# A three-layer transformer block on one core: the feed-forwards' first products computed by features, with the weights held stationary and 256 tokens moving

## The chip, the core and the metric

The kernel runs on one core of a Trainium2 chip. Five engines run side by side: PE (TensorE, matrix products into PSUM), DVE (VectorE) and ACT (ScalarE) for elementwise work, POOL (GpSimd) and SP (SyncE, which issues most DMAs here). They meet by semaphores alone. The metric is the time of one launch on the device, in microseconds (us). Several launches are timed and their median is given; one more launch was profiled.

## The reference

The input is 256 tokens of width 1024. Two layers of feed-forward, mixer (latent attention in one, forgetting attention in the other), feed-forward and gated embedding are followed by a block of dilated attention and pooling. The change touches the four feed-forwards alone:

```python
def rms_norm(x, g):
    y = x * lax.rsqrt(jnp.mean(x * x, axis=-1, keepdims=True) + EPS)
    return y * g

def swiglu(x, w_in, w_out):
    gate, up = jnp.split(x @ w_in, 2, axis=-1)
    return (jax.nn.silu(gate) * up) @ w_out

h = h + FFN_HALF * swiglu(rms_norm(h, g_ffn), w_in, w_out)   # w_in 1024 x 5632, w_out 2816 x 1024
```

Everything is in single precision. The kernel gets it from the fast format fp32r: each operand is split into a rounded part (hi) and the remainder (lo), and a product is the sum of hi·hi, hi·lo and lo·hi, three matmuls into one accumulator.

## The kernel before, in words

The program is written out by hand, engine by engine, with a table (`PLAN`) that numbers every weight group and every fill of an accumulator. Weights come in groups of 1 MB: SP fetches group g into `raw[:, g % 4]`, ACT rounds it into `wh` (L1328), DVE subtracts to get `wl` (L1809), and PE reads both. These two passes over each group run through the whole kernel in a ring of four slots.

A feed-forward (`ffn` on each engine) has 11 chunks of 256 gate and 256 up features, two groups each. The normalized input stands transposed in `xh` and `xl`: eight blocks of 128 features by 256 tokens. The row scale of the norm, `rstd`, one number per token, isn't in it; it is applied to the products.

For each chunk PE takes the tokens as the stationary operand (`tall_group`, L593 to L595):

```python
mm = products(acc(q, t)[:, 0:n], ah_[:, k0 + k, t * P:(t + 1) * P],
              al_[:, k0 + k, t * P:(t + 1) * P],
              wh[:, s, k * n:(k + 1) * n], wl[:, s, k * n:(k + 1) * n],
```

So 8 blocks x 2 token halves x 3 products = 48 matmuls stream 512 weight columns each, and `acc(q, t)` holds 128 tokens by 256 gate and 256 up values. ACT makes `sg` = silu(gate · rstd) per half (L1411), DVE makes `a_n` = up · rstd · sg (L1960). The second product needs `a_n` with features on the partitions, so in the middle of the next chunk PE turns it by four 128x128 transposes into `misc` (`turn_products`, L668); ACT rounds the result into `ah` (L1417) and DVE subtracts for `al` (L1967). After the last chunk the wide stage multiplies `ah` and `al` by `w_out` (L593 to L595 in its first chunk, then L626, L627, L630).

Accumulators alternate: chunk c+2 fills the banks of chunk c, after `acc_read` tells that DVE has read them. On DVE and ACT the order in a chunk is written out: split of a group, remainder (or rounding) of the chunk before, split of the next group, then the activation work, which waits for PE's end of the chunk. The first chunks are written out (3 in the first feed-forward, 1 in the others) and the rest run in a hardware loop of two chunks.

Elsewhere in the kernel there are fp32r matmuls with other numbers of moving columns: 288 and 384 in the latent attention, and 256 with a stationary operand of 16 columns for the forget gates (L1068, L1071, L1072).

Of the kernel before, what the change touches and what calls it, by code (L numbers as in the profile page):

```python
# [76 lines left out]
def plan():  # L77
# [1 line left out]

    sizes = {  # L80
        "norm": (0, 0, (1, 1, 1, 1), (4, 4, 4, 4)),
        "ffn": (33, 13, (6, 5, 0, 0), (6, 5, 0, 0)),
        "ffn_t": (33, 13, (6, 5, 0, G3), (6, 5, 0, G3)),
        "ffn_p": (33, 13, (6, 5, 1, 0), (6, 5, 1, 0)),
        "mla": (14, 12 + H, (H // 2 + 2, H // 2 + 2, H + 2, H + 1), (H + 2, H + 2, H + 2, H + 1)),
        "fox": (17, 9, (H, H, H, H + 3), (H, H, H, H + 3)),
        "ple": (5, 4, (0, 0, 0, 0), (0, 0, 0, 0)),
# [72 lines left out]
def build(nc, I, out):  # L160
    with ExitStack() as ctx:
# [182 lines left out]
        rstd_done = sem("rstd_done")  # L344
        xh_done = sem("xh_done")
        silu_done = sem("silu_done")
        ah_done = sem("ah_done")
        gate_done = sem("gate_done")
        lat_sq = sem("lat_sq")
# [40 lines left out]
        def acc_reads(q):  # L390

            return 2 * (q // 2) + 2
# [168 lines left out]

        TURN_AT = {"n1": 4}
        FIRST_SILU = {"f0": 0, "f1": 1, "f2": 2, "f3": 3}
        OH = {"mla": 0, "fox": 4, "b2": 4 + PAIRS}


        @block.tensor
        def _(pe):
# [146 lines left out]
            def ffn(name, nname, r, after, r_after, with_p=None):  # L715
# [13 lines left out]
                def turn_products(c, i=0):  # L729

                    b, q = c % 2, q0 + c
                    pe.wait_ge(acc_read[q % 2], acc_reads(q) + 2 * i)
                    if r0[b] + c // 2 > 0:
                        pe.wait_ge(m_read[b], r0[b] + c // 2 + i)
                    for t in range(NT):
                        for k in range(2):
                            mm = turn(b, slice(k * S + t * P, k * S + (t + 1) * P),
                                      a_n[:, b, t, k * P:(k + 1) * P])
                    mm.then_inc(m_ready[b], 1)

                peel = 3 if g0 == 0 else 1
                first_fill(nname, r, g0, q0)
                for c in range(1, peel):
                    chunk(c)
                with pe.Fori(0, (FCH - peel) // 2) as i:
                    for c in range(2):
                        chunk(peel + c, i)
                q, g = q0 + FCH, g0 + 2 * FCH
                for c in range(FCH):
                    wait_group(g + c)  # L750
                    pe.wait_ge(m_read[c % 2], r0[c % 2] + c // 2 + 1)
                    if c == 0:
                        wide_first(g, q, ah, al)
                    else:
                        for t in range(NT):
# [550 lines left out]
        def _(act):  # L1306
# [95 lines left out]
            def ffn(name, r):  # L1402
                g0, q0, f0, _ = PLAN[name]

                def silus(c, i=0):
                    q, g = q0 + c, g0 + 2 * c + 1
                    for t in range(NT):
                        tile_ready(act, q, t, g, i, 2)
                        if c == 0:
                            scaled(r, t)  # L1410
                        act.activation(sg[:, c % 2, t, :], acc(q, t)[:, 0:256], ACT.Silu,  # L1411
                                       scale=rstd[:, t:t + 1]).then_inc(silu_done, 1)

                def round_a(c, i=0):
                    b = c % 2
                    act.wait_ge(m_ready[b], f0[b] + c // 2 + 1 + i)
                    act.activation(ah[:, bass.ds(i * 4 + 2 * c, 2), :],  # L1417
                                   M[:, b, :].rearrange("p (k n) -> p k n", k=2), ACT.Copy).then_inc(ah_done, 1)

                peel = 3 if g0 == 0 else 1  # L1420
                for c in range(peel):
                    split_to(g0 + 2 * c + 3)
                    if c:
                        round_a(c - 1)
# [6 lines left out]
                with act.Fori(0, (FCH - peel) // 2) as i:  # L1431
                    for c in range(peel, peel + 2):
# [355 lines left out]
        def _(dve):  # L1788
# [161 lines left out]

            def ffn(name, r, after):

                g0, q0, f0, _ = PLAN[name]
                base = FIRST_SILU[name] * FCH

                def gated(c, i=0):
                    q = q0 + c
                    for t in range(NT):
                        dve.wait_ge(silu_done, NT * (base + c) + t + 1 + 4 * i)
                        dve.scalar_tensor_tensor(a_n[:, c % 2, t, :], acc(q, t)[:, 256:512], rstd[:, t:t + 1],  # L1960
                                                 sg[:, c % 2, t, :], ALU.mult, ALU.mult)\
                           .then_inc(acc_read[q % 2], 1)

                def rest_a(c, i=0):
                    b = c % 2
                    dve.wait_ge(ah_done, base + c + 1 + 2 * i)
                    dve.tensor_tensor(al[:, bass.ds(i * 4 + 2 * c, 2), :], pair(M[:, b, :]),  # L1967
                                      ah[:, bass.ds(i * 4 + 2 * c, 2), :].bitcast(F32), ALU.subtract)\
                       .then_inc(m_read[b], 1)

                peel = 3 if g0 == 0 else 1
                for c in range(peel):
                    split_to(g0 + 2 * c + 3)
                    if c:
                        rest_a(c - 1)
# [4 lines left out]
                with dve.Fori(0, (FCH - peel) // 2) as i:  # L1980
                    for c in range(peel, peel + 2):
# [775 lines left out]
```

## Time and profile before

| what | value |
|---|---|
| median of 3 launches | 1351.64 us (1349.71 to 1352.4) |
| the profiled launch's own time | 1351.75 us |
| its span in the trace | 1349.9 us |
| PE busy | 1325.5 us, 98% of the span, 6514 matmuls |
| weight loads of PE (PEld) | 1092.0 us, 6514 |
| DVE busy | 789.1 us, 58% |
| ACT busy | 672.6 us, 50% |
| DMA | 236.46 MB, 175 GB/s on average |
| granted TensorE clock, mean | 0.997 |

The durations of matmuls are modelled and overlap each other, so PE's speed is read from the distance between the starts of neighbours, not from "busy" or from the mean length of one. PEld is the loading of the stationary operand, which runs beside the matmul before it. A line of the code is that of the helper in which the instruction is made: L593 to L595 are every "three products" of the kernel, L668 is every transpose, and the names tell them apart.

### The profile page before, as it was taken

The numbers are of one execution on the slowest core, as the hardware profiler recorded it, in microseconds if no ns is written. First come the engines' busy times: TensorE is split into PE (matmuls) and PEld (weight loads), VectorE is DVE, ScalarE is ACT, GpSimd is POOL, SyncE is SP. The second block draws the span as 40 slices with busy tenths as digits, with TensorE's granted clock in tenths as the row PEclk, the third lists the DMA queues.
The fourth block names the chain that finished last, engine by engine and source line by source line (L and its number), as shares of the span: only waits on it lengthen the run. The fifth ranks groups of instructions, "written<-read, shape, count | busy, mean of one in ns | idle before, by whom it ended". The sixth has DMA issues, their size and how long they took to land.

```text
span 1349.9 us, 17526 instructions
## 1 busy us (share of the span) xinstructions
PE 1325.5 (98%) x6514; PEld 1092.0 (81%) x6514; DVE 789.1 (58%) x1013; ACT 672.6 (50%) x945; POOL 148.2 (11%) x207
## 2 busy tenths in 40 slices
PE   9999999899999999999999999999999999999996
PEld 6888788788888887888888788888888788888875
DVE  6655548875555546655545566655554645655663
ACT  7444427756444436544434555544443735457441
POOL 2000003811000000000001230000000132110500
PEclk9999999999999999999999999999999999999999
DMA  9655545235655654555554643465564495545531
GB/s 301 211 186 186 187 153 181 79 128 179 190 184 186 220 176 156 185 183 187 184 197 156 219 156 123 135 187 186 186 218 157 156 303 176 160 133 172 186 126 32
DMA packets 148782, 236.46 MB, mean 175 GB/s; under 512 B 10087, under 2 KB 103447, under 8 KB 148208
## 3 DMA queue, kind: packets, MB, share of 16 engines
q1 hardware_dynamic: 143680, 222.52, 50.6%
q0 software_dynamic: 4736, 12.96, 3.2%
q8 instruction: 40, 0.66, 0.2%
q10 hardware_dynamic: 304, 0.14, 0.1%
q14 instruction: 22, 0.18, 0.0%
HBM read 233.43 MB, written 4.51 MB: 176 GB/s over the span
## 4 chain that ended last, share of the span: by engine, by line
PE 85%; DVE 7%; ACT 3%; issue 2%; DMA 1%; POOL 1%; SPq 0%; POOLq 0%; DVEq 0%; ACTq 0%
PE acc L593 19%; PE acc L595 18%; PE acc L594 18%; PE acc L626 7%; PE acc L627 7%; PE acc L630 7%; PE misc L668 5%; DVE wl L1809 2%; ACT wh L1328 1%; ACT xh L1372 1%; PE misc L1018 1%; DMA decay<-decay_rows 1%; PE misc L1186 1%; DVE xl L1853 1%; PE misc L1205 1%
## 5 line engine op out<-in xcount | busy, mean ns | idle before, releaser
L1809 DVE TENSOR_TENSOR wl<-raw,wh 128x2048 fp32r<-128x2048 f32 (+2 forms) x203 | 458.7, 2267 | 265.6 <-ACT wh L1328 265.5
L1328 ACT ACTIVATE wh<-raw 128x2048 fp32r<-128x2048 f32 (+2 forms) x207 | 388.9, 1890 | 138.7 <-PE acc L630 130.3
L593 PE MATMUL acc<-wh,xh 128*128 128x512 f32 (+1 forms) x832 | 328.9, 395 | 2.7 <-DVE xl L1853 1.4
L595 PE MATMUL acc<-wh,xl 128*128 128x512 f32 (+1 forms) x832 | 323.2, 388 | 0.0
L594 PE MATMUL acc<-wl,xh 128*128 128x512 f32 (+1 forms) x832 | 322.6, 388 | 0.0
L593 PEld LDWEIGHTS acc<-wh,xh 128*128 128x128 f32 x832 | 156.3, 188 | 36.6 <-DVE wl L1802 4.2
L595 PEld LDWEIGHTS acc<-wh,xl 128*128 128x128 f32 x832 | 156.2, 188 | 32.7
L594 PEld LDWEIGHTS acc<-wl,xh 128*128 128x128 f32 x832 | 156.5, 188 | 30.0
L626 PE MATMUL acc<-wh,ah 128*128 128x512 f32 x320 | 125.7, 393 | 0.0
L627 PE MATMUL acc<-wl,ah 128*128 128x512 f32 x320 | 124.6, 389 | 0.0
L2541 POOL TENSOR_SCALAR rstd<-ssq 128x1 f32<-128x1 f32 x20 | 9.5, 476 | 905.2 <-ACT hn L1360 905.1
L1417 ACT ACTIVATE ah<-misc 128x512 f32 (+1 forms) x44 | 26.3, 598 | 156.0 <-PE misc L668 156.0
L593 PE MATMUL acc<-wh,zh 128*128 128x512 f32 x256 | 102.8, 401 | 0.8 <-DVE zl L1853 0.8
L595 PE MATMUL acc<-wh,zl 128*128 128x512 f32 x256 | 100.4, 392 | 0.0
L594 PE MATMUL acc<-wl,zh 128*128 128x512 f32 x256 | 100.2, 392 | 0.0
L630 PE MATMUL acc<-wh,al 128*128 128x512 f32 x320 | 98.6, 389 | 0.0
L1411 ACT ACTIVATE sg<-acc,rstd 128x256 f32<-128x256 f32 x88 | 41.4, 475 | 100.6 <-PE acc L595 100.6
L1967 DVE TENSOR_TENSOR al<-misc,ah 128x512 f32 (+1 forms) x44 | 30.4, 692 | 84.0 <-ACT ah L1417 84.0
L1372 ACT ACTIVATE xh<-misc,gains 128x128 fp32r<-128x128 f32 x128 | 40.3, 364 | 69.2 <-PE misc L668 60.1
L626 PEld LDWEIGHTS acc<-wh,ah 128*128 128x128 f32 x320 | 60.1, 188 | 13.8 <-issue 1.7
L630 PEld LDWEIGHTS acc<-wh,al 128*128 128x128 f32 x320 | 60.1, 188 | 12.7
L627 PEld LDWEIGHTS acc<-wl,ah 128*128 128x128 f32 x320 | 60.1, 188 | 12.2
(346 smaller groups left out, 1688.3 us busy)
## 6 DMA issues: line engine op xcount, KB each, us to landing
raw<-in_ffn_w_in_dram SPq DMA_DIRECT2D x172, 512.0 KB, 4.7
raw<-in_ffn_w_out_dram SPq DMA_DIRECT2D x88, 512.0 KB, 4.4
raw<-in_w_in_dram SPq DMA_DIRECT2D x64, 512.0 KB, 4.8
raw<-in_fox_w_in_dram SPq DMA_DIRECT2D x24, 512.0 KB, 4.5
raw<-in_ple_w_gate_dram SPq DMA_DIRECT2D x16, 512.0 KB, 4.1
raw<-in_mla_w_o_dram SPq DMA_DIRECT2D x8, 512.0 KB, 4.4
raw<-in_fox_w_o_dram SPq DMA_DIRECT2D x8, 512.0 KB, 4.4
raw<-in_w_out_dram SPq DMA_DIRECT2D x8, 512.0 KB, 4.5
```

What stands on the lines that cost most here:

```text
L593: pe.matmul(dst, hi, rhs_h, start=first, stop=False)
L594: pe.matmul(dst, hi, rhs_l, start=False, stop=False)
L595: return pe.matmul(dst, lo, rhs_h, start=False, stop=last)
L626: pe.matmul(acc(q + n, t), xa, wh[:, s, r], start=st, stop=False)
L627: pe.matmul(acc(q + n, t), xa, wl[:, s, r], start=False, stop=False)
L630: mm = pe.matmul(acc(q + n, t), xb, wh[:, s, r], start=False, stop=en)
L668: return pe.transpose(M[0:rows, b, cols], src, m[:, :])
L1328: act.activation(wh[:, s, 0:n], raw[:, s, 0:n], ACT.Copy).then_inc(hi_done, 1)
L1372: act.activation(x_cols(xh, r, k, t), turned(r, k, t), ACT.Copy, scale=gains[:, c:c + 1]).then_inc(xh_done, 1)
L1411: act.activation(sg[:, c % 2, t, :], acc(q, t)[:, 0:256], ACT.Silu, scale=rstd[:, t:t + 1]).then_inc(silu_done, 1)
L1809: dve.tensor_tensor(wl[:, s, 0:n], raw[:, s, 0:n], wh[:, s, 0:n].bitcast(F32), ALU.subtract)\
L1967: dve.tensor_tensor(al[:, bass.ds(i * 4 + 2 * c, 2), :], pair(M[:, b, :]), ah[:, bass.ds(i * 4 + 2 * c, 2), :].bitcast(F32), ALU.subtract)\
```

## The change

In each feed-forward, chunk 0 stays as it was. Chunks 1 to 10 swap the operands: a 128x128 block of `wh` or `wl` is stationary and `xh` or `xl` streams its 256 tokens. `acc(q, 0)` then holds 256 gate features (two blocks of 128) by 256 tokens and `acc(q, 1)` the up features, so the products already stand as the second product needs them. The row scale lies along the moving direction now. PE makes a row of it once per feed-forward, as two matmuls of `rstd`, broadcast to 128 columns, with the identity; DVE copies that to `rrow`. DVE scales the gate into `sg`, ACT takes the silu of `sg` in place, DVE scales the up part into `a_n` and multiplies the two; `ah` and `al` come from `a_n` directly. All four feed-forwards write out three chunks ahead of the loop on PE, ACT and DVE.

```diff
-        "ffn": (33, 13, (6, 5, 0, 0), (6, 5, 0, 0)),
+        "ffn": (33, 13, (1, 1, 0, 0), (1, 1, 0, 0)),
...
+        PEEL = 3
+        rrow = hn[:, 0, 0:S]
...
                 def chunk(c, i=0):
                     q, g = q0 + c, g0 + 2 * c
                     open_acc(q, i)
-                    for k in range(2):
-                        wait_group(g + k, i)
-                        tall_group(g + k, q, xh, xl, 4 * k, 4, 512, k == 0, k == 1)
-                        if k == 0:
-                            turn_products(c - 1, i)
+                    for n in range(2):
+                        wait_group(g + n, i)
+                        s = (g + n) % RING
+                        for k in range(4):
+                            x = 4 * n + k
+                            for b in range(4):
+                                dst = acc(q, b // 2)[:, (b % 2) * S:(b % 2 + 1) * S]
+                                w = slice(512 * k + P * b, 512 * k + P * (b + 1))
+                                pe.matmul(dst, wh[:, s, w], xh[:, x, :], start=x == 0 and b % 2 == 0, stop=False)
+                                pe.matmul(dst, wh[:, s, w], xl[:, x, :], start=False, stop=False)
+                                mm = pe.matmul(dst, wl[:, s, w], xh[:, x, :], start=False,
+                                               stop=x == DK - 1 and b % 2 == 1)
+                                if x == DK - 1 and b == 1:
+                                    mm.then_inc(acc_ready, 1)
+                        mm.then_inc(w_used, 1)
+                        if c == 1 and n == 0:
+                            turn_products()
+                            scales_by_token()
...
+                def scales_by_token():
+                    pe.wait_ge(rstd_done, NT * r + NT)
+                    open_m(1, r0[1])
+                    for t in range(NT):
+                        mm = pe.matmul(M[:, 1, t * P:(t + 1) * P], rstd[:, t:t + 1].to_broadcast([P, P]), ident[:, :],
+                                       start=True, stop=True)
+                    mm.then_inc(m_ready[1], 1)
...
-                    if c == 0:
-                        turn_products(FCH - 1)
...
 # ACT
+                    if c:
+                        act.wait_ge(gate_scaled, at + c + 2 * i)
+                        act.activation(sg[:, c % 2, :, :], sg[:, c % 2, :, :], ACT.Silu).then_inc(silu_by_feature, 1)
+                        return
...
+                    if c:
+                        act.wait_ge(a_done, at + c + 2 * i)
+                        act.activation(ah[:, bass.ds(i * 4 + 2 * c, 2), :], a_n[:, c % 2, :, :], ACT.Copy)\
+                           .then_inc(ah_done, 1)
+                        return
...
 # DVE
+                    if c == 1:
+                        dve.wait_ge(m_ready[1], f0[1] + 1)
+                        dve.tensor_copy(rrow, M[:, 1, 0:S]).then_inc(m_read[1], 1)
+                        dve.wait_ge(m_read[1], r0[1] + 1)
+                    tile_ready(dve, q, 0, g0 + 2 * c + 1, i, 2)
+                    dve.tensor_tensor(sg[:, c % 2, :, :], pair(acc(q, 0)), by_block, ALU.mult).then_inc(gate_scaled, 1)
+                    tile_ready(dve, q, 1, g0 + 2 * c + 1, i, 2)
+                    dve.tensor_tensor(a_n[:, c % 2, :, :], pair(acc(q, 1)), by_block, ALU.mult)\
+                       .then_inc(acc_read[q % 2], 2)
+                    dve.wait_ge(acc_read[q % 2], acc_reads(q) + 2 * i)
+                    dve.wait_ge(silu_by_feature, at + c + 2 * i)
+                    dve.tensor_tensor(a_n[:, c % 2, :, :], a_n[:, c % 2, :, :], sg[:, c % 2, :, :], ALU.mult)\
+                       .then_inc(a_done, 1)
...
+                    if c:
+                        dve.tensor_tensor(lo, a_n[:, c % 2, :, :], hi, ALU.subtract).then_inc(al_done, 1)
```

How it stands on PE in the middle of chunk 1 of a feed-forward, before (L668 turns the products of chunk 0):

```order
L595 MATMUL acc<-wh,xl 128x512
L668 MATMUL misc<-ident,a_n 128x128 x4
L593 MATMUL acc<-wh,xh 128x512
L594 MATMUL acc<-wl,xh 128x512
L595 MATMUL acc<-wh,xl 128x512
```

and of the change, at the same place (names are stationary last: `acc<-xh,wh` has `wh` stationary):

```order
L748 MATMUL acc<-xh,wl 128x256
L682 MATMUL misc<-ident,a_n 128x128 x4
L772 MATMUL misc<-ident,rstd 128x128 x2
L746 MATMUL acc<-xh,wh 128x256
L747 MATMUL acc<-xl,wh 128x256
L748 MATMUL acc<-xh,wl 128x256
```

The four transposes stand in every chunk from 1 on before, and once more in the wide stage; of the change they stand here alone, with two matmuls for the scale row behind them, and a chunk holds 96 matmuls of 256 columns in place of 48 of 512.

How it stands on DVE in one chunk of the loop, before:

```order
L1809 TENSOR_TENSOR wl<-raw,wh 128x2048 [waits hi_done]
L1966 REGISTER_ALU
L1967 ISA [waits ah_done]
L1967 TENSOR_TENSOR al<-misc,ah 128x512
L1808 REGISTER_ALU
L1809 TENSOR_TENSOR wl<-raw,wh 128x2048 [waits hi_done]
L1960 SCALAR_TENSOR_TENSOR a_n<-acc,rstd,sg 128x256 [waits silu_done] x2
```

and of the change:

```order
L1849 TENSOR_TENSOR wl<-raw,wh 128x2048 [waits hi_done]
L2025 ISA [waits ah_done]
L2025 TENSOR_TENSOR al<-a_n,ah 128x512
L1848 REGISTER_ALU
L1849 TENSOR_TENSOR wl<-raw,wh 128x2048 [waits hi_done]
L403 REGISTER_ALU
L2011 TENSOR_TENSOR sg<-acc,hn 128x512 [waits acc_ready]
L2013 TENSOR_TENSOR a_n<-acc,hn 128x512 [waits w_used]
L2015 REGISTER_ALU
L2017 TENSOR_TENSOR a_n<-a_n,sg 128x512 [waits silu_by_feature,acc_read0]
```

The two gated products of 256 elements have become three operations of 512, and the last of them waits for ACT, which itself waits for the first; the splits stand where they stood.

## Rows read from the trace of the kernel before

**Rows 1.** The page: busy time by engine, and the chain that ended last, by engine.

```profile
PE 1325.5 (98%) x6514; PEld 1092.0 (81%) x6514; DVE 789.1 (58%) x1013; ACT 672.6 (50%) x945; POOL 148.2 (11%) x207
...
PE acc L593 19%; PE acc L595 18%; PE acc L594 18%; PE acc L626 7%; PE acc L627 7%; PE acc L630 7%; PE misc L668 5%; DVE wl L1809 2%; ACT wh L1328 1%; ACT xh L1372 1%; PE misc L1018 1%; DMA decay<-decay_rows 1%; PE misc L1186 1%; DVE xl L1853 1%; PE misc L1205 1%
```

**Rows 2.** Timeline of PE, loop of feed-forward 0: start us, length us, line, op, names, count.

```profile
60.85 0.39 PE L595 MATMUL acc<-wh,xl 128*128 128x512 f32 x1
61.08 0.60 PE L668 MATMUL misc<-ident,a_n 128*128 128x128 f32 x4
...
61.75 0.39 PE L594 MATMUL acc<-wl,xh 128*128 128x512 f32 x1
...
83.81 0.60 PE L668 MATMUL misc<-ident,a_n 128*128 128x128 f32 x4
```

**Rows 3.** Timeline of PE, 512 moving columns: first and last of 29 in a row.

```profile
99.73 0.39 PE L593 MATMUL acc<-wh,xh 128*128 128x512 f32 x1
...
106.08 0.39 PE L594 MATMUL acc<-wl,xh 128*128 128x512 f32 x1
```

**Rows 4.** Timeline of PE, 384 columns (39 in a row) in latent attention.

```profile
227.03 0.33 PE L593 MATMUL acc<-wh,lh 128*128 128x384 f32 x1
...
233.62 0.33 PE L595 MATMUL acc<-wh,ll 128*128 128x384 f32 x1
```

**Rows 5.** Timeline of PE, 288 columns: second and last of 36 in a row.

```profile
202.16 0.29 PE L594 MATMUL acc<-wl,xh 128*128 128x288 f32 x1
...
206.69 0.29 PE L595 MATMUL acc<-wh,xl 128*128 128x288 f32 x1
```

**Rows 6.** Timeline of PE, forget gates: 256 columns, 16 stationary, first and last of 24.

```profile
733.62 0.28 PE L1068 MATMUL acc<-xh,wh 128*16 128x256 f32 x1
...
736.31 0.28 PE L1072 MATMUL acc<-xh,wl 128*16 128x256 f32 x1
```

**Rows 7.** Timeline of weight loads (PEld) in the last block's attention.

```profile
1225.74 1.86 PEld L1209 LDWEIGHTS misc<-qkv,pT 128*128 128x128 f32 x16
```

**Rows 8.** Groups by form: count | busy us, mean ns of one | idle before.

```profile
L1809 DVE TENSOR_TENSOR wl<-raw,wh 128x2048 fp32r<-128x2048 f32 x196 | 448.7, 2297 | 259.2 <-ACT wh L1328 259.1
...
L594 PEld LDWEIGHTS acc<-wl,xh 128*128 128x128 f32 x832 | 156.5, 188 | 30.0
...
L1960 DVE SCALAR_TENSOR_TENSOR a_n<-acc,rstd,sg 128x256 f32<-128x256 f32 x88 | 42.1, 483 | 26.8 <-ACT sg L1411 26.8
...
L1967 DVE TENSOR_TENSOR al<-misc,ah 128x512 f32 x38 | 26.3, 692 | 75.8 <-ACT ah L1417 75.8
...
L1417 ACT ACTIVATE ah<-misc 128x512 f32 x38 | 22.7, 598 | 137.4 <-PE misc L668 137.4
...
L1817 DVE TENSOR_TENSOR wl<-raw,wh 128x512 fp32r<-128x512 f32 x12 | 8.1, 678 | 0.0
```

**Rows 9.** Busy time by engine in one chunk: us, PE, PEld, DVE, ACT, POOL (counts), clock, DMA.

```profile
55.70:67.00 11.30, 11.30 (x54) 9.35 (x53) 6.21 (x5) 5.16 (x5) 0.00 (x0) 1.00 0.62 192
```

**Rows 10.** Timeline of DVE over a chunk of the loop; idle before in brackets.

```profile
79.07 0.48 DVE L1960 SCALAR_TENSOR_TENSOR a_n<-acc,rstd,sg 128x256 f32<-128x256 f32 x1 [0.20 <-ACT sg L1411]
80.87 2.29 DVE L1809 TENSOR_TENSOR wl<-raw,wh 128x2048 fp32r<-128x2048 f32 x1 [1.32 <-ACT wh L1328]
...
89.74 0.48 DVE L1960 SCALAR_TENSOR_TENSOR a_n<-acc,rstd,sg 128x256 f32<-128x256 f32 x1 [0.48 <-ACT sg L1411]
```

**Rows 11.** Timeline of DVE behind chunk 1 of feed-forward 0.

```profile
34.04 0.87 DVE L1960 SCALAR_TENSOR_TENSOR a_n<-acc,rstd,sg 128x256 f32<-128x256 f32 x2
...
36.73 2.29 DVE L1809 TENSOR_TENSOR wl<-raw,wh 128x2048 fp32r<-128x2048 f32 x1
```

**Rows 12.** Timeline of PE in the middle of chunk 2 of feed-forward 0.

```profile
38.70 0.48 PE L593 MATMUL acc<-wh,xh 128*128 128x512 f32 x1
```

**Rows 13.** The page: the queue that fetches PE's instructions.

```profile
q8 instruction: 40, 0.66, 0.2%
```

**Rows 14.** Chain of waits, in order of time: start us, us, what.

```profile
528.80 1.58 issue
```

More of the change, by code:

```diff
@@ L346, in build @@
         silu_done = sem("silu_done")
+        gate_scaled = sem("gate_scaled")
+        silu_by_feature = sem("silu_by_feature")
+        a_done = sem("a_done")
+        al_done = sem("al_done")
         ah_done = sem("ah_done")
@@ L735, in turn_products @@
+                def turn_products():
+                    pe.wait_ge(acc_read[q0 % 2], acc_reads(q0))
+                    open_m(0, r0[0])
                     for t in range(NT):
                         for k in range(2):
[L737 to L741, printed above, removed]
+                            mm = turn(0, slice(k * S + t * P, k * S + (t + 1) * P), a_n[:, 0, t, k * P:(k + 1) * P])
+                    mm.then_inc(m_ready[0], 1)
@@ L742, in ffn @@
+                def scales_by_token():
[5 more added lines that the diff above has]
+                    mm.then_inc(m_ready[1], 1)
                 first_fill(nname, r, g0, q0)
-                for c in range(1, peel):
+                for c in range(1, PEEL):
@@ L744, in ffn @@
                     chunk(c)
-                with pe.Fori(0, (FCH - peel) // 2) as i:
+                with pe.Fori(0, (FCH - PEEL) // 2) as i:
                     for c in range(2):
-                        chunk(peel + c, i)
+                        chunk(PEEL + c, i)
                 q, g = q0 + FCH, g0 + 2 * FCH
@@ L1430, in ffn @@
                         act.activation(cs[:, :, :, :], rc[:, :, :, :], ACT.Sin).then_inc(sines, 1)
-                with act.Fori(0, (FCH - peel) // 2) as i:
-                    for c in range(peel, peel + 2):
+                with act.Fori(0, (FCH - PEEL) // 2) as i:
+                    for c in range(PEEL, PEEL + 2):
                         split(g0 + 2 * c + 2, i)
@@ L1951, in ffn @@
             def ffn(name, r, after):
-                g0, q0, f0, _ = PLAN[name]
-                base = FIRST_SILU[name] * FCH
+                g0, q0, f0, r0 = PLAN[name]
+                base, at = FIRST_SILU[name] * FCH, by_feature(name)
+                by_block = rrow.unsqueeze(1).to_broadcast([P, 2, S])
                 def gated(c, i=0):
                     q = q0 + c
[L1958 to L1962, printed above, removed]
+                    if c == 0:
+                        for t in range(NT):
+                            dve.wait_ge(silu_done, NT * FIRST_SILU[name] + t + 1)
+                            dve.scalar_tensor_tensor(a_n[:, 0, t, :], acc(q, t)[:, 256:512], rstd[:, t:t + 1],
+                                                     sg[:, 0, t, :], ALU.mult, ALU.mult)\
+                               .then_inc(acc_read[q % 2], 1)
+                        return
+                    if c == 1:
[11 more added lines that the diff above has]
+                       .then_inc(a_done, 1)
@@ L1964, in rest_a @@
                 def rest_a(c, i=0):
-                    b = c % 2
                     dve.wait_ge(ah_done, base + c + 1 + 2 * i)
[L1967 to L1972, printed above, removed]
+                    hi = ah[:, bass.ds(i * 4 + 2 * c, 2), :].bitcast(F32)
@@ L1973, in ffn @@
+                    lo = al[:, bass.ds(i * 4 + 2 * c, 2), :]
+                    if c:
+                        dve.tensor_tensor(lo, a_n[:, c % 2, :, :], hi, ALU.subtract).then_inc(al_done, 1)
+                    else:
+                        dve.tensor_tensor(lo, pair(M[:, 0, :]), hi, ALU.subtract).then_inc(m_read[0], 1)
+                for c in range(PEEL):
                     split_to(g0 + 2 * c + 3)
@@ L1979, in ffn @@
                         (angles_reduced, head_constants, rope_tables)[c]()
-                with dve.Fori(0, (FCH - peel) // 2) as i:
-                    for c in range(peel, peel + 2):
+                with dve.Fori(0, (FCH - PEEL) // 2) as i:
+                    for c in range(PEEL, PEEL + 2):
                         split(g0 + 2 * c + 2, i)
```

33 lines of the change are left out of this document (14 added, 19 removed).

## The prediction

> **What bounds the kernel now.** I read the page first: PE is busy for 98% of the span and DVE for 58%, and the chain that ended last is almost only PE's lines, products first and transposes (L668) with 5% [rows 1]. So an edit in the feed-forwards counts by what it does to PE's time there, as long as DVE and ACT stay hidden. Second, the timeline of PE in a loop: turns of products follow each other two chunks apart at 61.08 and 83.81 us, which makes 11.365 us a chunk [rows 2], and no idle time stands beside them. Third, the cadence of matmuls, start to start. 28 steps of 512 columns take 6.35 us, 226.8 ns each [rows 3]. Fourth, the same for narrower ones, since the change issues 256. Last, DVE and ACT in one chunk: 6.21 and 5.16 us of work in 11.3 us [rows 9].
>
> **Part 1: transposes removed.** From the last matmul before a turn (60.85) to the second behind it (61.75) are 0.90 us [rows 2]; two steps of 0.227 would be 0.454, so four transposes cost PE 0.446 us, all of it on the path. Each feed-forward has 11 such turns and keeps one. 40 x 0.446 = 17.8 us go.
>
> **Part 2: the products.** Chunks 1 to 10 of four feed-forwards have 40 x 48 = 1920 matmuls of 512 columns and get 40 x 96 = 3840 of 256. The streamed columns are the same. What isn't the same is the piece of a step that doesn't scale with columns. Three forms with a full 128-column stationary operand show it:
> - 512 columns: 226.8 ns [rows 3]
> - 384 columns: 6.59 us over 38 steps, 173.4 ns [rows 4]
> - 288 columns: 4.53 us over 34 steps, 133.2 ns [rows 5]
>
> From 512 down to 384 the slope is 0.417 ns a column, on to 288 0.419; 32 columns less give 133.2 - 13.4 = 119.8 ns at 256. No column is saved, and some 13 ns of fixed cost are paid twice as often. No row has 256 fp32r columns on 128 stationary ones, so I bound it. From below: the forget gates stream 256 columns of the same `xh` and `xl` over only 16 stationary columns, 23 steps in 2.69 us, 117.0 ns [rows 6]; a full weight load can't be cheaper. From above: 16 weight loads of 128 columns stand in 1.86 us where the matmuls between are short; less the last one's 0.19, 15 steps of 111.5 ns are what a stream of loads takes by itself [rows 7]. That is under 119.8, so loads alone don't bind. If the 13.1 ns that 119.8 stands over its columns (256 at 0.417, 106.7) came on top of the load instead of the columns, it would be 111.5 + 13.1 = 124.6. The length of a load record, 188 ns [rows 8], is no bound: the same loads already follow each other every 133.2 ns [rows 5]. I take 119.8, since it is the same kind of instruction and the extrapolation is over 32 columns.
>
> A chunk is then 96 x 0.1198 = 11.50 us against 11.365 with its transposes: +0.136 us, over 40 chunks +5.4 us.
>
> The Trainium skill has a rule here, "TensorE: Matmul & The Clock Gate", section "Back-to-back issue gap": an isolated step takes N/2.4 + 2.5 ns. By it a 256-column step would be 109.2 ns. The trace disagrees already at 512 columns (215.8 by the rule, 226.8 measured) and at 256 with a small load (109.2 against 117.0), so the measured cadence decides; it is among the rivals below for what it would do.
>
> **Part 3: the scale row.** Two matmuls per feed-forward in the code, in plain fp32. Such a matmul runs as two: L1209 makes 8 calls at a time, and rows 7 show 16 loads. At the 0.112 us of rows 7 each, that is 4 x 4 x 0.112 = 1.8 us on PE. The copy to `rrow` is DVE's.
>
> **Part 4: DVE and ACT.** DVE's chunk before is 2 x 2.297 + 2 x 0.483 + 0.692 = 6.25 us [rows 8], 6.21 by the window [rows 9]. Now two scalings out of PSUM (0.692 each, like L1967), a product and a remainder from SBUF (0.678, like L1817): 4.59 + 1.38 + 1.36 = 7.3 us of 11.5. ACT trades two silus and a rounding for one of each over 512, about 0.6 each: no more than its 5.16. Both are costed at nothing; their cover is PE's 11.5 us, and without it the extra 1.1 us of DVE would be 44 us over 40 chunks.
>
> The new handoff is DVE, ACT, DVE at a chunk's end. Before, the last gated product ends about 1.2 us behind PE (a second half at 79.07 + 0.48 where the chunk ends near 78.35), and the next split starts at 80.87 only because ACT's does [rows 10]. Now: gate scaled while PE finishes the up part, silu 0.6, up scaled 0.69, product 0.68: done some 1.9 us behind PE, and the split behind it is again held by ACT's. The split that PE needs at the next chunk but one start is over 6 us early, so nothing reaches PE. The banks are free about 1 us after the chunk; they are wanted a whole chunk later, in the wide stage after its first 12 matmuls, 2.7 us.
>
> The tightest place is feed-forward 0, where DVE also makes constants. Behind chunk 1 its gated work is 0.87 us at 34.04 and the next split starts at 36.73 [rows 11]. The row copy (up to 0.5), two scalings, the wait for the silu and the product make it about 3.2, so that split ends near 41.3 in place of 39.02. Chunk 3 needs it at 38.70 + 24 x 0.227 + 0.09 = 44.2 [rows 12]. Hidden by 3 us. SP's fetches follow the splits; the group of 1 MB that they bring is wanted no faster than before.
>
> **Sum.** 5.4 + 1.8 = +7.2 us on the profiled launch's 1351.75: 1359.0. The median of the launches is 0.1 lower, so 1358.9 us. As a formula, with s the 256-column step in ns: 3.84 s - 452.8 us. It is zero at 117.9 ns; one nanosecond is 3.84 us. A measurement of this kernel can tell about 0.2%, 2.7 us, so steps of 117.2 to 118.6 ns give no difference.
>
> **Rivals.**
> - *A, the step is cheaper (117.0 to 117.2 ns), faster.* The place is PE's step in chunks 1 to 10; the fixed cost would shrink as the streaming part does. For it: the 117.0 of rows 6, and that 14 ns over the columns at 512 (226.8 - 213.3) are 13.4 at 384 and 13.2 at 288, so it falls a little. Against: rows 6 has a load of 16 columns. At 117.0: -3.5 us, 1348.1. It decides from 117.9 down. Chance 0.12, with whatever else the removed transposes set free. With a step of 109.2, the figure of the Trainium skill's TensorE page cited above, the time would be 33 us less, 1318; the two measured steps leave that 1 in 100 of these 12.
> - *B, between,* 117.2 to 118.6: 1349 to 1354.3. Chance 0.13.
> - *C, the weight load or its issue becomes the bound,* 124.6 ns: +25.7 us, 1377.3. For it: loads and streams are now both near 107 to 112 ns, so neither hides much of the other, and no row has more than 24 such steps in a row. Against: rows 7 hold 111.5 with full loads. Chance 0.05.
> - *D, the loop's branch costs.* The loop body on PE is 384 loads and matmuls in place of 208. For: a longer way back. Against: 0.66 MB of instructions were fetched in 40 packets [rows 13] while 13028 loads and matmuls ran, so loops weren't fetched again. The Trainium skill, "Runtime: NRT & Kernel Launch", section "Instruction fetch mechanics", says that a taken branch to a page no longer held stalls, but that PE holds 2048 instructions; no run here shows the size. At a stall like the longest "issue" piece of the chain between two DVE steps, 1.58 us [rows 14], 16 iterations give +25 more: 1384. Chance 0.03.
> - *E, the handoff reaches PE,* in feed-forward 0 or where a bank opens: it decides once DVE is over 3 us later than worked out; 1 us in each feed-forward gives 1363, 1 us in each chunk 1399. Chance 0.02.
>
> **How the numbers follow.** The forecast, a step of 118.6 to 121.5, has 0.65 and its own range of 1354.3 to 1365.4. Slower by over 0.2%: 0.65 + 0.05 + 0.03 + 0.02 = 0.75. Within 0.2%: B, 0.13. Faster: A, 0.12. The range of 8 in 10 takes in the forecast, B and the near end of E, together 0.79: 1349 to 1366; A lies below, C and D above.
>
> **What would show it.** In the profile after: 6514 - 160 transposes + 1920 + 16 = 8290 matmuls. The starts of neighbouring 256-column matmuls stand 119.8 ns apart; 117 says A, 125 C. Chunks are 11.5 us apart, without a gap at their borders. L668's share for `a_n` falls to four groups of four; their PE time of 17.8 us is gone. DVE's share rises to about 61%: 40 x 1.1 us. ACT stays near 50%. An idle PE before a chunk's first matmul, released by DVE, says E; a gap every second chunk, released by nothing, says D. I am wrong if PE's time in ten chunks is not near 115 us.

## The result and the profile after

| | before | changed |
|---|---|---|
| median of 4 launches each | 1350.7 us | 1359.46 us |
| lowest and highest | 1349.71 to 1352.4 | 1358.39 to 1360.04 |
| span of the profiled execution | 1349.9 us | 1357.3 us |

The ratio is 1.0063, with a 95% interval of 1.0048 to 1.0078: slower, by more than the 0.2% that can be told from nothing. By the medians the change costs 8.8 us, by the ratio 8.5. The forecast was 1358.9 us. The first lines are the page's, busy time by engine and the chain that ended last; they answer to [rows 1], and the fetch queue's line to [rows 13].

```profile
PE 1333.4 (98%) x8290; PEld 1178.5 (87%) x8290; DVE 828.5 (61%) x1057; ACT 656.5 (48%) x905; POOL 147.5 (11%) x207
...
q8 instruction: 48, 0.79, 0.2%
...
PE acc L746 11%; PE acc L747 11%; PE acc L748 11%; PE acc L607 8%; PE acc L609 8%; PE acc L608 8%; PE acc L640 7%; PE acc L641 7%; PE acc L644 7%; PE misc L682 3%; DVE wl L1849 2%; ACT wh L1362 1%; ACT xh L1406 1%; PE misc L1052 1%; PE misc L1220 1%
```

PE is busy for the same 98% and stays the bound; the transposes' share of the chain (L668 before, L682 now) falls from 5% to 3%. The three products of the new form (L746 to L748) have 11% each. Their groups, by line, with busy us, mean ns of one, and idle time before them, and DVE's first operation of a chunk, which waits for PE:

```profile
L746 PE MATMUL acc<-xh,wh 128*128 128x256 f32 x1280 | 362.6, 283 | 0.2 <-DVE wl L1849 0.2
L748 PE MATMUL acc<-xh,wl 128*128 128x256 f32 x1280 | 362.2, 283 | 0.0
L747 PE MATMUL acc<-xl,wh 128*128 128x256 f32 x1280 | 362.2, 283 | 0.0
...
L2011 DVE TENSOR_TENSOR sg<-acc,hn 128x512 f32<-128x512 f32 x40 | 27.7, 692 | 113.2 <-PE acc L748 113.2
```

PE's whole idle time before 3840 matmuls is 0.2 us. What the change costs is therefore in the distance between starts, which the timeline of PE shows (start, length, line), against [rows 3]:

```profile
99.74 0.28 PE L748 MATMUL acc<-xh,wl 128*128 128x256 f32 x1
99.86 0.28 PE L746 MATMUL acc<-xh,wh 128*128 128x256 f32 x1
...
106.94 0.28 PE L748 MATMUL acc<-xh,wl 128*128 128x256 f32 x1
```

From 99.74 to 106.94 are 60 steps in 7.20 us: 120.0 ns. Of all 3832 steps between two such matmuls 3823 lie between 117 and 120, with a mean of 120.0. Five are of 0.20 to 0.22 us, at the first matmul of all and behind each scale row; with them the mean is 120.1. Two of them stream the columns that one step of 226.8 ns streamed before. So a chunk of 96 takes 11.52 us, against 11.365 before: 48 x 0.2268 = 10.89 us of products and 0.48 us for its turn. Of these 0.48, 0.446 are those of the prediction. The rest lies behind the turn, where the trace of before has nine steps of 512 at 228 to 234 ns on the mean until 226.7 is reached again.

The same shows as a lag between the two traces, read at matmuls that both kernels have (of a group, the count is what the window held; its start is what matters). Before:

```profile
13.91 0.50 PE L593 MATMUL acc<-wh,xh 128*128 128x512 f32 x1 [0.18 <-DVE wl L1802]
...
152.07 0.92 PE L775 MATMUL misc<-onehot,rb 33*8 33x448 f32 x2
...
539.27 0.49 PE L668 MATMUL misc<-ident,h 128*128 128x128 f32 x3
...
719.56 0.51 PE L668 MATMUL misc<-ident,h 128*128 128x128 f32 x3
```

and after:

```profile
13.28 0.51 PE L607 MATMUL acc<-wh,xh 128*128 128x512 f32 x1
...
153.38 0.92 PE L809 MATMUL misc<-onehot,rb 33*8 33x448 f32 x2
...
544.39 0.38 PE L682 MATMUL misc<-ident,h 128*128 128x128 f32 x2
...
726.66 0.50 PE L682 MATMUL misc<-ident,h 128*128 128x128 f32 x3
```

| feed-forward | lag ahead of its chunks 1 to 10, us | lag behind them, us | added |
|---|---|---|---|
| 0 | 13.28 - 13.91 = -0.63 | 153.38 - 152.07 = 1.31 | 1.94 |
| 1 | 324.65 - 321.55 = 3.10 | 453.90 - 448.76 = 5.14 | 2.04 |
| 2 | 544.39 - 539.27 = 5.12 | 726.66 - 719.56 = 7.10 | 1.98 |
| 3 | 859.62 - 852.87 = 6.75 | 1073.28 - 1064.48 = 8.80 | 2.05 |

Each feed-forward adds 2.0 us, 8.0 in all. The lag also moves outside the changed chunks. It starts at -0.63, since in the profiled launch of before PE waited for the split of the first weights (the row at 13.91), ahead of anything that was changed. It grows by 0.4 in the first mixer and falls by 0.35 in the second, which is left open. And each trace has one stretch of 3.4 us with a granted clock of 0.50, the lower of its two levels (1.2 GHz), at another place. The windows show the busy us of PE, PEld, DVE, ACT and POOL with their counts, then the granted clock, the share of DMA and its GB/s, in the first mixer of the changed kernel and at the start of the last block in the kernel before:

```profile
254.27:257.68 3.41, 3.41 (x15) 2.67 (x15) 2.29 (x8) 1.77 (x7) 2.65 (x3) 0.50 0.04 15
...
1069.46:1072.87 3.41, 3.15 (x8) 2.51 (x9) 3.41 (x14) 3.41 (x13) 0.00 (x0) 0.50 0.00 0
```

Ahead of each stretch, PE had short matmuls with idle time between them: 0.73 us of work in the last 1.60 us there, 1.29 in the last 3.41 here. Each stretch costs its kernel 1.4 to 1.5 us by the lag (from 1.66 to 3.10 at 250 to 266 us, from 8.80 to 7.34 at 1068 to 1074 us), so the two cancel in the spans. A single launch of a kernel can have such a stretch or not, which is worth remembering below where 1 or 2 us are compared.

The middle of chunk 1, where one turn and the scale row stand, on PE:

```profile
26.50 0.28 PE L748 MATMUL acc<-xh,wl 128*128 128x256 f32 x1
26.62 0.60 PE L682 MATMUL misc<-ident,a_n 128*128 128x128 f32 x4
27.05 0.61 PE L772 MATMUL misc<-ident,rstd 128*128 128x128 f32 x4
27.42 0.36 PE L746 MATMUL acc<-xh,wh 128*128 128x256 f32 x1
27.62 0.28 PE L747 MATMUL acc<-xl,wh 128*128 128x256 f32 x1
```

From 26.50 to 27.62 are 1.12 us. Less two steps of 0.120 and the turn's 0.446, the scale row has 0.43 us for its four, 0.109 each and 1.7 us in all.

DVE over a chunk of the loop, idle before in brackets; it answers to [rows 10]:

```profile
78.82 0.69 DVE L2011 TENSOR_TENSOR sg<-acc,hn 128x512 f32<-128x512 f32 x1 [3.23 <-PE acc L748]
79.61 0.69 DVE L2013 TENSOR_TENSOR a_n<-acc,hn 128x512 f32<-128x512 f32 x1
80.33 0.69 DVE L2017 TENSOR_TENSOR a_n<-a_n,sg 128x512 f32<-128x512 f32 x1
82.01 2.29 DVE L1849 TENSOR_TENSOR wl<-raw,wh 128x2048 fp32r<-128x2048 f32 x1 [0.99 <-ACT wh L1362]
...
90.34 0.69 DVE L2011 TENSOR_TENSOR sg<-acc,hn 128x512 f32<-128x512 f32 x1 [3.23 <-PE acc L748]
```

DVE now waits 3.23 us for PE's gate part in each chunk: it has room. The window of one chunk, in the same order as the windows above, against [rows 9]:

```profile
56.00:67.50 11.50, 11.50 (x98) 11.50 (x98) 7.15 (x7) 4.76 (x4) 0.00 (x0) 1.00 0.81 258
```

### The profile page after: what moved, and what is told of

It reads as the page before. It is cut to its first block, busy times and chain, and to the rows that moved or that the text cites. A ratio compares the mean times of both kernels' runs of the same rounds, so it can differ in the third digit from the quotient of the medians.

```text
span 1357.3 us, 20978 instructions
## 1 busy us (share of the span) xinstructions
PE 1333.4 (98%) x8290; PEld 1178.5 (87%) x8290; DVE 828.5 (61%) x1057; ACT 656.5 (48%) x905; POOL 147.5 (11%) x207
## 4 chain that ended last, share of the span: by engine, by line
PE 87%; DVE 6%; ACT 3%; issue 2%; DMA 0%; POOL 0%; SPq 0%; POOLq 0%; DVEq 0%; ACTq 0%
PE acc L746 11%; PE acc L747 11%; PE acc L748 11%; PE acc L607 8%; PE acc L609 8%; PE acc L608 8%; PE acc L640 7%; PE acc L641 7%; PE acc L644 7%; PE misc L682 3%; DVE wl L1849 2%; ACT wh L1362 1%; ACT xh L1406 1%; PE misc L1052 1%; PE misc L1220 1%
## 5 line engine op out<-in xcount | busy, mean ns | idle before, releaser
L746 PE MATMUL acc<-xh,wh 128*128 128x256 f32 x1280 | 362.6, 283 | 0.2 <-DVE wl L1849 0.2
L748 PE MATMUL acc<-xh,wl 128*128 128x256 f32 x1280 | 362.2, 283 | 0.0
L747 PE MATMUL acc<-xl,wh 128*128 128x256 f32 x1280 | 362.2, 283 | 0.0
L746 PEld LDWEIGHTS acc<-xh,wh 128*128 128x128 f32 x1280 | 245.7, 192 | 0.7 <-DVE wl L1849 0.6
L747 PEld LDWEIGHTS acc<-xl,wh 128*128 128x128 f32 x1280 | 245.7, 192 | 0.1
L748 PEld LDWEIGHTS acc<-xh,wl 128*128 128x128 f32 x1280 | 245.7, 192 | 0.0
L641 PE MATMUL acc<-wl,ah 128*128 128x512 f32 x320 | 124.6, 389 | 0.0
L2011 DVE TENSOR_TENSOR sg<-acc,hn 128x512 f32<-128x512 f32 x40 | 27.7, 692 | 113.2 <-PE acc L748 113.2
L607 PE MATMUL acc<-wh,xh 128*128 128x512 f32 (+1 forms) x192 | 75.9, 395 | 2.0 <-DVE xl L1893 1.3
L609 PE MATMUL acc<-wh,xl 128*128 128x512 f32 (+1 forms) x192 | 73.5, 383 | 0.0
L608 PE MATMUL acc<-wl,xh 128*128 128x512 f32 (+1 forms) x192 | 73.3, 382 | 0.0
```

Source lines behind the costliest of these rows:

```text
L607: pe.matmul(dst, hi, rhs_h, start=first, stop=False)
L608: pe.matmul(dst, hi, rhs_l, start=False, stop=False)
L609: return pe.matmul(dst, lo, rhs_h, start=False, stop=last)
L641: pe.matmul(acc(q + n, t), xa, wl[:, s, r], start=False, stop=False)
L746: pe.matmul(dst, wh[:, s, w], xh[:, x, :], start=x == 0 and b % 2 == 0, stop=False)
L747: pe.matmul(dst, wh[:, s, w], xl[:, x, :], start=False, stop=False)
```

## The experiments

Two theories stood behind the runs. **Columns and a fixed piece:** a step takes its columns at 0.417 ns and some 13 ns more, and the load is hidden; a step is only dear because there are twice as many. **Loads:** a 128-column load is what a 256-column step waits for, and fewer columns gain nothing. Where a ratio is given, its kernel was timed in rounds against the kernel before on the same chip; the others are one launch, so their times are good to 1 or 2 us, and the steps in their traces say more.

### The two halves of the change apart

**e1**, the kernel before with each turn made twice:

```diff
-                    for t in range(NT):
-                        for k in range(2):
+                    for _ in range(2):
+                        for t in range(NT):
+                            for k in range(2):
```

> The kernel before, with each turn of products made twice (44 x 4 more transposes, PE only). Theory (a turn costs PE 0.446 us, all on the path, four transposes of 0.109 and a little at the border): 44 x 0.436 = +19.2 us, ratio 1.014. Rival (part of a turn hides in waits that PE has anyway): less than half of that, under +10 us.

Measured: 1369.36 us against 1349.79, ratio 1.0141 (1.0124 to 1.0158), +19.6 us by the medians and 19.0 by the ratio, where 19.2 was expected. The timeline of PE:

```profile
61.93 0.40 PE L595 MATMUL acc<-wh,xl 128*128 128x512 f32 x1
62.16 1.04 PE L668 MATMUL misc<-ident,a_n 128*128 128x128 f32 x8
...
63.27 0.39 PE L594 MATMUL acc<-wl,xh 128*128 128x512 f32 x1
```

1.34 us less two steps of 0.227 are 0.886 for eight transposes, twice 0.443. From turn to turn a chunk takes 11.79 us on the mean in place of 11.365. Nothing of a turn is hidden, so the 17.8 us did go.

**e2**, the changed kernel with four transposes put back into the middle of chunks 2 to 10, their result unused:

```diff
+                        if c > 1 and n == 0:
+                            pe.wait_ge(m_read[0], r0[0] + 1)
+                            for j in range(4):
+                                turn(0, slice(j * P, (j + 1) * P), ident[:, :])
```

> The changed kernel, with four dummy transposes of the identity in the middle of chunks 2 to 10, so PE keeps the swapped operands and gets most of its removed transposes back. Theory (the change is the sum of -0.446 us a turn and +0.6 us a chunk from the 256-column steps): 36 x 0.446 = +16 us on the changed kernel, about 1375.5 us, so the swapped operands alone cost +25 us on the kernel before, ratio 1.018. Rival (the transposes stand where PE has slack between short steps): under +8 us.

Measured: 1375.43 us, ratio 1.0187 (1.017 to 1.0204) to the kernel before, +16.0 us on the changed one: 36 x 0.44. The timeline of PE shows the same 0.44 (0.68 us from 111.46 to 112.14, less two steps of 0.120):

```profile
111.46 0.28 PE L748 MATMUL acc<-xh,wl 128*128 128x256 f32 x1
111.58 0.60 PE L682 MATMUL misc<-ident 128*128 128x128 f32 x4
111.94 0.36 PE L746 MATMUL acc<-xh,wh 128*128 128x256 f32 x1
112.14 0.28 PE L747 MATMUL acc<-xl,wh 128*128 128x256 f32 x1
```

So this kernel, with 40 chunks of swapped operands and 40 of the 44 turns, is 25.6 us slower than the one before. By steps: 40 x (11.52 - 10.89) = 25.2, the scale row 1.7, four turns fewer -1.8: 25.1. The swap costs about 25 us and its scale row 1.7; the missing turns give back 40 x 0.48 = 19, of which 18 are in the turns themselves and 1 is in the steps behind them.

### What a 256-column step consists of

**e3**, the second and third product stream 240 of the 256 tokens:

```diff
-                                pe.matmul(dst, wh[:, s, w], xl[:, x, :], start=False, stop=False)
-                                mm = pe.matmul(dst, wl[:, s, w], xh[:, x, :], start=False,
+                                pe.matmul(dst[:, 0:240], wh[:, s, w], xl[:, x, 0:240], start=False, stop=False)
+                                mm = pe.matmul(dst[:, 0:240], wl[:, s, w], xh[:, x, 0:240], start=False,
```

> The changed kernel, where the second and third product of a block stream only the first 240 of 256 tokens (the low parts of 16 tokens are left out). Theory (a step is its columns at 2.4 GHz plus 13.3 ns, 120.0 at 256): steps behind a 240-column matmul 113.3 ns, 2560 x 6.7 = -17 us, about 1342. Rival (the 120.0 is that of the weight load, 128 columns, or of its issue): still 120, no change in time.

Measured: 1336.01 us, 23 less than the changed kernel. The timeline of PE:

```profile
100.05 0.28 PE L746 MATMUL acc<-xh,wh 128*128 128x256 f32 x1
100.17 0.28 PE L747 MATMUL acc<-xl,wh 128*128 128x240 f32 x1
100.28 0.27 PE L748 MATMUL acc<-xh,wl 128*128 128x240 f32 x1
100.39 0.28 PE L746 MATMUL acc<-xh,wh 128*128 128x256 f32 x1
```

The means of the steps (here and below without the five long ones) are 119.8, 111.0 and 111.9 ns, 342.7 for three, where the loads' theory had 360 and mine 346.7. Columns do count at 256. But 16 of them took off 8 to 9 ns, where 0.417 a column makes 6.7: here my theory was already off. (The 23 us and the 22 that the steps make, 1277 x 17.3 ns, agree within the scatter of single launches.)

**e4**, the same with 192 tokens (the same two lines with 0:192).

> As the one with 240, with 192 columns in the second and third product (the low parts of 64 tokens are left out). Theory: the columns would allow 93.3 ns, but weight loads follow each other at 111.5 at best, so steps of 111 to 112 ns, 2560 x 8.5 = -22 us, about 1338. Rival with no floor of loads: 93 ns, -68 us. Rival with the load as the bound already at 256: 120, no change.

Measured: 1335.35 us, no more than e3 although 48 columns less are streamed twice in three. Means 140.6, 90.7 and 109.9 ns, 341.2 for three, 113.7 each. The 96 columns less in three steps gained 1.5 ns on e3, so a floor is reached, some 2 ns over the 111.5 of [rows 7], and e3 with 114.2 each was already near it. In the timeline of PE the step behind a 256-column matmul has grown by what the shorter ones had saved:

```profile
100.33 0.31 PE L746 MATMUL acc<-xh,wh 128*128 128x256 f32 x1
100.48 0.26 PE L747 MATMUL acc<-xl,wh 128*128 128x192 f32 x1
100.57 0.27 PE L748 MATMUL acc<-xh,wl 128*128 128x192 f32 x1
100.68 0.30 PE L746 MATMUL acc<-xh,wh 128*128 128x256 f32 x1
```

**e5**, all 256 tokens, but the second product loads only 64 of its 128 stationary columns:

```diff
-                                pe.matmul(dst, wh[:, s, w], xl[:, x, :], start=False, stop=False)
+                                v = slice(w.start, w.start + 64)
+                                pe.matmul(dst[0:64], wh[:, s, v], xl[:, x, :], start=False, stop=False)
```

> The changed kernel, where the second product of a block holds only 64 of 128 stationary columns (the wh-xl part of 64 features in each block is left out); all three still stream 256 columns. Theory (a step of 256 is bound by its columns, and its 13.3 ns are fixed): the step to and from the half load stays within 117 to 120 ns, under -4 us in all, 1356 to 1359. Rival (loads bind at 256, as the 113.8 ns a step of the kernel with 192 columns makes thinkable): the step that waits for the half load drops towards 107, -12 us or more.

Measured: 1345.16 us, 14 less than the changed kernel: this one spoke against my theory. The timeline of PE:

```profile
100.71 0.28 PE L746 MATMUL acc<-xh,wh 128*128 128x256 f32 x1
100.82 0.28 PE L748 MATMUL acc<-xl,wh 128*64 128x256 f32 x1
100.94 0.28 PE L749 MATMUL acc<-xh,wl 128*128 128x256 f32 x1
101.05 0.28 PE L746 MATMUL acc<-xh,wh 128*128 128x256 f32 x1
```

Means 116.3, 115.0 and 118.8 ns, 350.1 for three against 360. The columns are the same, so a part of the step belongs to the load. At 256 columns neither theory holds alone: fewer columns shorten the step, and so does a smaller load. It fits the 117.0 of [rows 6], where the load had 16 columns.

**e9**, the changed kernel with the twelve matmuls of a feature block in another order, so that no two neighbours share a stationary block or a bank:

```diff
-                            for b in range(4):
...
+                            for j in range(3):
+                                for b in (0, 2, 1, 3):
...
```

> The changed kernel, with the twelve matmuls of a feature block in another order: each goes to another bank than the one before it, and neighbours never share a stationary block. Theory (13.3 ns a step over the columns belong to every pair of load and stream): steps of 120.0 as before, about 1359. Rival (they come from three products in a row that add into the same addresses, or from loading the same block twice): steps of 117 or less, 3840 x 3 = -11 us or more.

Measured: 1358.16 us, and its 3832 steps again have a mean of 120.0 ns. It is neither the accumulation into the same addresses nor the loading of the same block twice; 120 ns goes with any pair of a full load and 256 columns here.

### A version that keeps the transposes away and the long streams

If steps are what is dear, `xh` and `xl` can pass the same stationary block of `wh` in one matmul of 512 columns. That makes 64 steps a chunk instead of 96.

**e6** does that for chunks 2 to 10. The low half lands in a bank of its own (the misc banks serve even chunks); ACT copies it out and DVE adds it. The scale row comes from two transposes:

```diff
+        xhl = sb("xhl", [P, 2, DK, S], F32R)
...
+                                low = lambda: pe.matmul(bank(c, b)[:, 0:S], wl[:, s, w], xh[:, x, :],
+                                                        start=False, stop=False)
...
+                                mm = pe.matmul(bank(c, b).rearrange("p (u n) -> p u n", u=2), wh[:, s, w],
+                                               xhl[:, :, x, :], start=x == 0, stop=x == DK - 1)
...
+                        act.activation(sg[:, c % 2, :, :], halves(c, 0)[1], ACT.Copy).then_inc(low_out, 1)
...
+                        half_sum(sg[:, c % 2, :, :], gh, sg[:, c % 2, :, :]).then_inc(gate_sum, 1)
```

> A version that keeps the swapped operands but loads a third less: in chunks 2 to 10 one block of wh is loaded once and streams xh and xl as 512 columns into a bank of its own, wl streams xh (256) into its first half; ACT copies the low half out, DVE adds it, four more operations of 512 a chunk. The misc banks serve the even chunks. The scale row comes from two transposes. Theory (cost per weight load is 13.3 ns whatever streams): a block is 226.7 + 120.0 = 346.7 ns in place of 360, a chunk 11.09 us in place of 11.52 and of 11.365 before; per feed-forward 9 x -0.27 + 0.155 + 0.22 = -2.1 us on the kernel before, -8 us in all, 1342, ratio 0.994. Rival 1 (the new work at a chunk's end reaches PE): PE idle before a chunk or before the wide stage, more than 1 us a feed-forward. Rival 2 (what costs is the switch between streams, not the load): a block of 360 or more, ratio over 1.0.

Measured: 1349.39 us against 1350.81, ratio 0.9994 (0.9985 to 1.0003): as fast as before, 9 us better than the changed kernel by the ratios, 7 short of what I had expected. No idle PE stands at the chunks' borders. The shortfall is in the steps:

```profile
100.11 0.39 PE L764 MATMUL acc<-xhl,wh 128*128 128x512 f32 x1
100.34 0.27 PE L760 MATMUL acc<-xhl,wl 128*128 128x256 f32 x1
100.45 0.40 PE L764 MATMUL acc<-xhl,wh 128*128 128x512 f32 x1
100.68 0.28 PE L760 MATMUL acc<-xhl,wl 128*128 128x256 f32 x1
```

A 512 ahead of a 256 takes 235.9 ns on the mean and a 256 ahead of a 512 takes 117.1: 353.0 a pair where 226.8 + 120.0 = 346.8 was expected.

**e7** puts the two halves next to each other in memory, since the 512 columns of e6 came in two stretches:

```diff
-        xhl = sb("xhl", [P, 2, DK, S], F32R)
+        xhl = sb("xhl", [P, DK, 2, S], F32R)
```

> As e6, with xh and xl of a feature block stored side by side, so the 512 moving columns are one stretch of memory and not two of 256 that lie 8 KB apart. e6 showed 235.9 ns for the 512 step and 117.1 for the 256 one, 353.0 a block. Theory (the second stretch of the operand costs the 9 ns; a plain 512 step is 226.8): a block is 344 to 347 ns, 36 x 32 x 7 = -8 us on e6, about 1341.5, ratio 0.993 to 0.994. Rival (the 236 come from changing between 512 and 256 steps or from the load, not from the two stretches): the step stays at 236 and the time at 1349.

Measured: 1349.38 us, ratio 0.9996 (0.9987 to 1.0005), again 235.9 and 117.1 ns. The theory of the second stretch fell.

**e8** issues four of 512 and then four of 256 for each feature block:

```diff
+                            for low in () if c == 1 else (True, False) if x == DK - 1 else (False, True):
+                                for b in range(4):
...
```

> As e7, with the order of a feature block changed: four 512-column matmuls, then four of 256, in place of one and one. Theory (the 6 ns a pair over 226.8 + 120.0 belong to the change of length from one matmul to the next): eight steps give 3 x 227 + 236 + 3 x 120 + 117 = 1394 ns in place of 1412, 288 x 18 = -5.2 us on e7, about 1344, ratio 0.996. Rival (they belong to each long or each short stream whatever its neighbours): 1412 again, 1349, ratio 1.000.

Measured: 1347.01 us against 1350.06, ratio 0.9975 (0.9964 to 0.9986). Half of the 5.2 us came back. But the dear steps aren't those at the change: a 512 ahead of a 256 takes 228.2 ns and a 256 ahead of a 512 118.5, while between neighbours of one length the steps are 232.8 and 118.7.

**e10** sorts a whole group, sixteen of 512 and then sixteen of 256, and the other way round in the second group:

```diff
-                            for low in () if c == 1 else (True, False) if x == DK - 1 else (False, True):
+                        for low in () if c == 1 else (n == 1, n == 0):
+                            for k in range(4):
...
```

> As e8, with a whole weight group in one go: 16 matmuls of 512, then 16 of 256 (the other way round in a chunk's second group). e8 showed 232.8 ns between 512-column neighbours and 118.7 between 256-column ones, about 350 a pair. Theory (the change of length disturbs some steps after it, so fewer changes leave 227 and 120): near 347 a pair, 288 x 4 x 2.5 = -3 us on e8, about 1344, ratio 0.9955. Rival (the long steps in this orientation are 231 to 233 wherever they stand, from the work of ACT and DVE beside them): 350 again, 1347, ratio 0.9975.

Measured: 1343.33 us against 1351.07, ratio 0.9948 (0.9934 to 0.9962). It is 7.0 us faster than the kernel before by the ratio (5.1 to 8.9), 7.7 by the medians, and about 15.5 faster than the change. The page and the timeline of PE:

```profile
PE 1316.8 (98%) x7130; PEld 1116.1 (83%) x7130; DVE 867.2 (65%) x1129; ACT 696.3 (52%) x977; POOL 148.4 (11%) x207
```

```profile
100.22 3.79 PE L764 MATMUL misc<-xhl,wh 128*128 128x512 f32 x16
103.84 4.00 PE L761 MATMUL misc<-xhl,wl 128*128 128x256 f32 x32
...
111.33 3.79 PE L764 MATMUL acc<-xhl,wh 128*128 128x512 f32 x16
```

A chunk is 111.33 - 100.22 = 11.11 us, with steps of 227.7 and 119.8 ns. By parts: 36 x (11.11 - 11.365) = -9.2, four chunks 1 at 11.52 +0.6, a scale row of two transposes in each feed-forward +0.9, so -7.7, within the measured interval.

The trace of e10 shows where the excess of a mixed order lies. Behind a stretch of 256-column matmuls the first five steps of 512 take 233, 236, 228, 232 and 231 ns on the mean, and from the sixth on every one is 226.7. Behind a stretch of 512 the first step of 256 takes 113 and the next 119, then 120.0. So a change there and back costs 27 - 8, about 20 ns, once, however long the stretches are, and e6 and e7, which change at every matmul, never get to 226.7. It is the same kind of tail that the kernel before has behind its turns. The rival of e10, that ACT and DVE beside it lengthen the 512s wherever they stand, falls with the 226.7. Why the steps behind a change are long stays open: the runs show that it goes with the order, not with the layout of the moving operand.

## Why the prediction was right

- **The bound.** Right: PE at 98% before and after, and the time moved by what PE's steps did.
- **Part 1, transposes.** Right in kind: 0.446 us a turn, 0.443 in e1 and 0.44 in e2, all on the path. Too small by 8% in size: a turn cost 0.48 us, with the long steps behind it, and 19 us went, not 17.8. The sum wasn't touched, since Part 2 took the whole chunk of 11.365 us.
- **Part 2, the 256-column step.** The value was right, 120.0 ns against 119.8, and 11.52 us a chunk against 11.50. The choice of the extrapolated line over the two bounds decided the case: the lower one (117.0) was 11 us away in the sum, the upper one (124.6) 18. Its reason was only partly right. "Loads alone don't bind" held (e3 went below 120), but "some 13 ns of fixed cost" is not fixed: the load has a share in it (e5), the step falls faster from 256 to 240 than above (e3), and below that is a floor of 113.7 ns (e4). Above 256 columns the line holds; that it still holds at 256, where the load already has a share and 16 columns less leave it, is luck as far as the working goes. Extended to 192 columns it would have given 93 ns.
- **Part 3, the scale row.** Right: sixteen matmuls, 1.7 us for 1.8.
- **Part 4, DVE and ACT.** Right: 7.15 us of DVE for 7.3 and 4.76 of ACT under 5.16. PE's chunk ends near 79.3 (its last one at 136.94, less five of 11.52) and the product at 81.02, 1.7 us behind where 1.9 was worked out; the next split waits for ACT. In feed-forward 0 the split behind chunk 1 ends at 40.1 where 41.3 was worked out, 4 us ahead of the 44.2 at which it was needed by the working; its rows on DVE:

```profile
35.32 0.69 DVE L2017 TENSOR_TENSOR a_n<-a_n,sg 128x512 f32<-128x512 f32 x1 [0.17 <-ACT sg L1444]
...
37.84 2.29 DVE L1849 TENSOR_TENSOR wl<-raw,wh 128x2048 fp32r<-128x2048 f32 x1
```

- **The sum.** +7.2 worked out. With the measured step it is 40 x (11.52 - 11.365) + 1.7 = +7.9, and the lags give 8.0. The spans differ by 7.4, because the profiled launch of before lost 0.6 at its first weights; the medians differ by 8.8, the ratio says 8.5 (6.5 to 10.5). So the sum was short by 1 us or so. That the time of 1359.46 came out 0.6 us from the forecast is partly luck: the forecast was built on launches with a median of 1351.64, and with one launch more that median is 1350.7.
- **The rivals.** A and B needed steps below 118.6 and had 120.0; e5 got there only with a smaller load. The step of 109.2 ns that was worked out from the Trainium skill's "TensorE: Matmul & The Clock Gate" (section "Back-to-back issue gap") is not seen in any feed-forward of the changed kernel. C had the right suspicion, a load with a share in the step, but adding the 13 ns on top of the load was wrong: 120.0, not 124.6. D: no gap at the loop's borders in 3832 steps, and 8 packets more fetched [rows 13], so the longer loop was not fetched again. E: PE's idle time before all 256-column matmuls is 0.2 us, once, before the first of them in feed-forward 0.

## What to carry over

Price a change of the stationary operand by counting its steps, each a load with its stream, and not columns alone. Moving the same columns in steps half as long cost 0.63 us a chunk here, more than the four transposes that the swap saved (0.48 us with the steps behind them). If a layout asks for short streams, look for operands that can share one load, as the high and low halves do in e10, and keep matmuls of one length together. An extrapolated step is worth what its nearest row is, so before going further down the line, find the floor of the loads.

## What was not expected of the chip

- Around 256 fp32r columns a step depends on both the stream and the load: 120.0 ns with 256 columns and a full load, 350.1 ns for three with one load halved, 342.7 for three with two streams at 240, 341.2 with them at 192. The Trainium skill, "TensorE: Matmul & The Clock Gate", section "LDWEIGHTS (loading the stationary operand)", gives P/1.2 ns for P columns, by which 128 would take an estimated 106.7; the floor of 113.7 ns a step in e4 and the 111.5 of [rows 7] lie 5 to 7 ns above it.
- Matmuls of 512 and 256 columns in turn took 353.0 ns a pair, and in sixteens 347 (11.11 us over the 32 pairs of a chunk). Over 36 chunks the 6 ns make 6.9 us; the ratios of e7 and e10 differ by 0.0048, 6.5 us. The excess lies in the first five steps of 512 behind a shorter kind.
- The four transposes of a turn cost PE 0.446 us in their own place and 0.04 us more in the nine steps of 512 behind them (228 to 234 ns in place of 226.7).
- Memory layout of a moving operand in two stretches or one made no difference: 235.9 and 117.1 ns both times.
- A stretch of 3.4 us at a granted clock of 0.50 cost either kernel 1.4 to 1.5 us, and stood in the first mixer in one trace and at the start of the last block in the other.
